# A Mamba-2 and mixture-of-experts layer on one core: moved loads, copies and waits at four joints between its stages

## The reference

```python
y = mamba2_mixer(x * (1 + sc1) + sh1, ...)             # ends in y_normed (2048 x 2048) @ w_out
x = layer_norm(ALPHA * x + (1 + g1) * y, g, b)
hm = x * (1 + sc2) + sh2
probs = softmax(hm @ w_router + b_router)              # 32 experts in 4 groups, the best group, its top 2
y = sum over the 2 chosen: gate * (silu(hm @ w_gate[e]) * (hm @ w_up[e])) @ w_down[e]
out = layer_norm(ALPHA * x + (1 + g2) * y, g, b)
```

## Time and profile before

| | |
|---|---|
| median of 3 runs | 2968.27 us (2964.40 to 2972.89) |
| profiled execution | 2967.99 us, span 2966.2 us, mean granted clock 0.973 |
| busy | PE 94%, PEld 79%, DVE 74%, POOL 49%, ACT 44% |
| mixer | to 1541 us |
| projection and norm | 1541 to 1933 us |
| router and tables | 1933 to 2010 us |
| experts | 2010 to 2870 us |
| output | 2870 to 2966 us |
| chain that ended last | PE 76%, DVE 11%, issue 4%, DMA 3% of the span |

### The profile page before, as it was taken

The page is one execution under the profiler, slowest core; times in us unless marked ns, Lnnn a source line. Parts: engine busy times, 40 slices in busy tenths (PEclk is TensorE's granted clock), DMA queues, the critical chain, the costliest instruction groups (busy, mean ns, idle before and its releaser), DMA issues.

```text
span 2966.2 us, 41186 instructions
## 1 busy us (share of the span) xinstructions
PE 2775.1 (94%) x14699; PEld 2333.7 (79%) x14699; DVE 2194.2 (74%) x2633; ACT 1309.1 (44%) x1671; POOL 1467.3 (49%) x753
## 2 busy tenths in 40 slices
PE   3899999999999999999988999948999999999986
PEld 2688888888888888888876888846888888888852
DVE  7678777787878778787764333385888888888867
ACT  4534333333433333343431111125777777777743
POOL 0133433333343343333432222214899999999974
PEclk9999999999999999999998999968999999999989
DMA  8854545444553544454352222239887869668768
GB/s 267 311 183 155 213 146 182 178 160 174 185 209 127 204 173 144 182 198 167 111 184 96 106 105 103 82 121 339 320 317 259 307 242 362 244 234 303 268 235 332
DMA packets 253183, 610.11 MB, mean 206 GB/s; under 512 B 15968, under 2 KB 98560, under 8 KB 244864
## 3 DMA queue, kind: packets, MB, share of 16 engines
q1 hardware_dynamic: 228208, 525.26, 49.6%
q0 software_dynamic: 11520, 41.95, 3.8%
q10 hardware_dynamic: 13328, 41.21, 3.4%
HBM read 600.75 MB, written 99.89 MB: 236 GB/s over the span
## 4 chain that ended last, share of the span: by engine, by line
PE 76%; DVE 11%; issue 4%; DMA 3%; POOL 2%; ACT 2%; SPq 1%; ACTq 0%; POOLq 0%; DVEq 0%
PE op L691 18%; PE pz L706 11%; PE op L1697 10%; PE gp_e L2124 9%; PE yp L2124 9%; PE up_e L2124 9%; DVE cv L1227 3%; PE yi L750 3%; PE yx L753 2%; PE op L2116 1%; PE sbp L758 1%; PE tx L769 1%; DVE decay L1264 1%; PE tx L723 1%; PE lgP L1722 1%
## 5 line engine op out<-in xcount | busy, mean ns | idle before, releaser
L2072 DVE TENSOR_TENSOR piece_lo<-piece_raw,piece_hi 128x2048 fp32r<-128x2048 f32 x186 | 552.1, 2987 | 119.8 <-ACT piece_hi L2181 119.7
L2181 ACT CAST piece_hi<-piece_raw 128x2048 fp32r<-128x2048 f32 x274 | 515.6, 1913 | 191.1 <-issue 78.9
L691 PE MATMUL op<-hm,w_hi 128*128 128x512 f32 x2048 | 532.3, 405 | 45.9 <-DVE hm L1353 45.9
L2072 POOL TENSOR_TENSOR piece_lo<-piece_raw,piece_hi 128x2048 fp32r<-128x2048 f32 x91 | 552.0, 6067 | 44.1 <-ACT piece_hi L2181 42.8
L1227 DVE SCALAR_TENSOR_TENSOR cv<-ub,par,cv 128x512 f32<-128x512 f32 x384 | 381.1, 993 | 154.0 <-ACT cv L950 144.8
L691 PEld LDWEIGHTS op<-hm,w_hi 128*128 128x128 f32 x2048 | 379.0, 190 | 120.1 <-DVE hm L1353 45.9
L641 POOL TENSOR_TENSOR xw<-xw,t 128x512 f32<-128x512 f32 x64 | 98.7, 1543 | 490.5 <-DVE t L1295 490.5
L706 PE MATMUL pz<-wz_hi,hm 128*128 128x256 f32 x2048 | 296.6, 290 | 1.1 <-DVE wz_lo L1205 0.4
L706 PEld LDWEIGHTS pz<-wz_hi,hm 128*128 128x128 f32 x2048 | 266.5, 192 | 7.3 <-DVE wz_lo L1205 3.9
L691 PE MATMUL op<-hm,w_lo 128*128 128x512 f32 x1024 | 254.9, 391 | 0.0
L622 POOL TENSOR_TENSOR xdt<-xw,tab 128x512 f32<-128x512 f32 x64 | 70.4, 1099 | 367.6 <-ACT xw L969 345.8
(11 more groups left out here) (344 smaller groups left out, 5755.3 us busy)
## 6 DMA issues: line engine op xcount, KB each, us to landing
hm<-hm_parts SPq DMA_DIRECT2D x30, 4096.0 KB, 14.0
piece_raw<-in_w_gate SPq DMA_DIRECT2D x94, 1024.0 KB
piece_raw<-in_w_up SPq DMA_DIRECT2D x94, 1024.0 KB
piece_raw<-in_w_down SPq DMA_DIRECT2D x92, 1024.0 KB
decay<-acum_rows SPq DMA_DIRECT2D x32, 1024.0 KB, 4.7
w_raw<-in_w_in SPq DMA_DIRECT2D x48, 512.0 KB, 6.0
expert_out<-ye ACTq DMA_DIRECT2D x46, 512.0 KB, 6.6
w_ada_part<-in_w_ada_t SPq DMA_DIRECT2D x32, 512.0 KB, 3.9
```

Of the source, the lines that this page charges most:

```text
L691: mm = nc.tensor.matmul(pj[m % 2][:], wp[m][:, kk, :], hm[b][:, hp, kk, :], start=q == 0, stop=q == 3 * KK - 1)
L2072: v.tensor_tensor(lo[q][:], raw[q][:], hi[q][:].bitcast(F32), ALU.subtract).then_inc(lo_done[q], 1)
L2181: nc.scalar.copy(hi[q][:], raw[q][:]).then_inc(hi_done[q], 1)
```

## The change

It has five edits.

1. SP issues `load_y(2, 0)` inside the mixer's list, behind the issue of the last y stores; step 1 of the projection loads only the second half. DVE runs `mix_rows` between the two low parts of tile 2.
2. ACT's `power(0, EARLY)` stands ahead of the wait for `lg_mm`.
3. DVE makes `ids`, `tile_expert` and `fresh` ahead of the low parts 3 and 4 of tile 0, and 3, 4 and 5 behind them.
4. The first two fetches gather by the column of `ids` itself, with no copy into `ix`; from tile 2 on the copy stays.
5. `xa` has 16 buffers, in the places of the raw and high pieces 0 to 3, `ya` moves to memory below. SP loads `xa1` to `xa8` as the low parts 0 to 3 of the tile behind the last come, and 9 to 15 behind these, and the output stage loads none. DVE waits for 8 to 15 once, at tile 8.

```diff
@@ output_buffers
+    w.ya = [sb(f"ya{n}", [P, D]) for n in range(OUT_RING)]
+    sb("unused14", [P, 440])
...
-    xa = [sb(f"xa{n}", [P, D]) for n in range(1, OUT_RING)]
+    xa = [sb(f"xa{n}", [P, D]) for n in range(1, TT)]
     sb("unused16", [P, D])
-    w.ya = [sb(f"ya{n}", [P, D]) for n in range(OUT_RING)]
...
+    w.xa_late = sem("xa_late")
@@ mixer_steps, sync
             store(LAST, 1)
+            for h in range(2):
+                sp.wait_ge(y_stored[h], 32 * (STEPS - SPANS + 2))
+            load_y(2, 0)
             sp.wait_ge(zero_out, 16 * GROUPS)
@@ out_projection, sync
-            if in_loop(i, 1, TT - 1):
+            if in_loop(i, 2, TT - 1):
                 load_y(i + 1, 0)
@@ out_projection, scalar
+                if isinstance(j, int) and j == TT - 2:
+                    power(0, EARLY)
                 if in_loop(j, 1, TT):
                     act.wait_ge(lg_mm, j)
-                if isinstance(j, int) and j == TT - 2:
-                    power(0, EARLY)
@@ out_projection, vector
-                low(i + 1, 1 - b)
+                low_half(i + 1, 1 - b, 0)
                 mix_rows()
+                low_half(i + 1, 1 - b, 1)
@@ experts, sync
-        for n in range(1, OUT_RING):
-
-            if n % 2:
-                sp.wait_ge(lo_done[(n - 1) // 2], 2 * last + 3)
-                sp.sem_inc(k.passed, 1)
-            sp.dma_start(w.xa[n][:], k.xad[n]).then_inc(w.xa_in[n], 16)
+        for q in range(GU):
+            sp.wait_ge(lo_done[q], 2 * last + 3)
+            sp.sem_inc(k.passed, 1)
+            for n in (2 * q + 1, 2 * q + 2):
+                sp.dma_start(w.xa[n][:], k.xad[n]).then_inc(w.xa_in[n] if n < OUT_RING else w.xa_late, 16)
+        for n in range(OUT_RING + 1, TT):
+            sp.dma_start(w.xa[n][:], k.xad[n]).then_inc(w.xa_late, 16)
@@ experts, gpsimd, fetch
-            nc.gpsimd.tensor_copy(ix[b][:], k.ids[:, bass.ds(t, 1)]).then_inc(ix_ready, 1)
-            pool.wait_ge(ix_ready, t + 1)
-            pool.sem_inc(k.passed, 1)
+                nc.gpsimd.tensor_copy(ix[b][:], k.ids[:, bass.ds(t, 1)]).then_inc(ix_ready, 1)
+                pool.wait_ge(ix_ready, t - 1)
+                pool.sem_inc(k.passed, 1)
+            rows = ix[b][:] if in_loop(t, 2) else k.ids[:, t:t + 1]
@@ experts, vector
-        low_part(dve, nc.vector, 3, 0)
-        low_part(dve, nc.vector, 4, 0)
         dve.wait_ge(ids_mm, 1)
...
-        low_part(dve, nc.vector, 5, 0)
+        for q in range(3, PIECES):
+            low_part(dve, nc.vector, q, 0)
@@ output, sync
-            if i + R < TT:
-                load(i + R)
@@ output, vector
-            dve.wait_ge(xa_in[s], 16 * (i // R + 1))
+            if i < R:
+                dve.wait_ge(xa_in[i], 16)
+            elif i == R:
+                dve.wait_ge(w.xa_late, 16 * (TT - R))
```

More of the change, by code:

```diff
@@ L265, in output_buffers @@
     w.ve = sb("ve2", [P, 1])
-    sb("unused14", [P, 11192 - 2 * D - 4 * P])
+    w.ya = [sb(f"ya{n}", [P, D]) for n in range(OUT_RING)]
+    sb("unused14", [P, 440])
     w.dga, w.dgb = ([sb(f"{n}{b}", [P, P]) for b in range(2)] for n in ("diag_a", "diag_b"))
@@ L2080, in fetch @@
                 pool.sem_inc(k.passed, 1)
-            nc.gpsimd.tensor_copy(ix[b][:], k.ids[:, bass.ds(t, 1)]).then_inc(ix_ready, 1)
-            pool.wait_ge(ix_ready, t + 1)
-            pool.sem_inc(k.passed, 1)
+                nc.gpsimd.tensor_copy(ix[b][:], k.ids[:, bass.ds(t, 1)]).then_inc(ix_ready, 1)
+                pool.wait_ge(ix_ready, t - 1)
+                pool.sem_inc(k.passed, 1)
+            rows = ix[b][:] if in_loop(t, 2) else k.ids[:, t:t + 1]
             nc.gpsimd.indirect_dma_start(out=xg[b][:], out_offset=None, in_=k.h2d[:],
-                                         in_offset=bass.IndirectOffsetOnAxis(ap=ix[b][:], axis=0)
+                                         in_offset=bass.IndirectOffsetOnAxis(ap=rows, axis=0)
                                          ).then_inc(x_in[b], 16)
@@ L2373, in _ @@
     def _(sp):
-        def load(i):
-            sp.wait_ge(r_done, i - R + 1)
-            sp.dma_start(xa[i % R][:], k.xad[i]).then_inc(xa_in[i % R], 16)
         for i in range(TT):
@@ L2452, in summed @@
         def summed(i):
-            s, b = i % R, i % 2
+            b = i % 2
             dve.wait_ge(ms_done, i + 1)
-            dve.wait_ge(xa_in[s], 16 * (i // R + 1))
+            if i < R:
+                dve.wait_ge(xa_in[i], 16)
+            elif i == R:
+                dve.wait_ge(w.xa_late, 16 * (TT - R))
             if i >= 2:
@@ L2458, in summed @@
                 dve.wait_ge(nm_done, i - 1)
-            nc.vector.tensor_tensor_reduce(out=r[b][:], in0=both[b][:], in1=xa[s][:], scale=1.0, scalar=0.0,
+            nc.vector.tensor_tensor_reduce(out=r[b][:], in0=both[b][:], in1=xa[i][:], scale=1.0, scalar=0.0,
                                            op0=ALU.add, op1=ALU.add, accum_out=total[b][:]).then_inc(r_done, 1)
```

## The result

The changed kernel takes 2943.82 us (median of 4 runs, 2941.0 to 2945.99) against 2969.73 for the kernel before beside it (4 runs, 2964.4 to 2972.89): ratio 0.9914, 95% interval 0.9896 to 0.9932. The forecast was 2933, with 2943 as the end of its range, so the sign was right and the gain was too large: 35.5 us forecast, 25.9 measured. The profiled execution took 2942.14 us with a span of 2940.4, against 2967.99 and 2966.2 before.

The account below looks back on a forecast made before the run. TensorE was taken as busy throughout the projection and expert loops, with waits or transfers binding four other stretches. Gains of 10.8 + 9.0 + 6.7 + 9.0 = 35.5 us from 2967.99 gave 2933 us, range 2926 to 2943.

Parts of the forecast that it names:

- Part 1: Mixer's end: earlier load of y for tile 2 gains 10.8 us; bounds 9.0, and 12.6 if tile 3's slow start goes.
- Part 2: Router: exponential waits only for its own input, gaining 9.0 us (8.0 to 9.6); the rest becomes a wait for x.
- Part 3: First gather at the experts' start: earlier token table and no index copy give 6.85 us together, taken as 6.7.
- I expect it 0.8 us ahead of the first low part: Experts' start: GpSimd's first gather issue begins 0.8 us before VectorE's first low part, keeping the 6.7 us gain.
- GpSimd's first gather is locked out: Rival at the experts' start: the first gather gains 3.7 us instead of 6.7, total 2936 us; chance 8%.
- lower bound of 3.7 us: Experts' start: gain left if the first gather's issue falls behind one low part, starting at about 1999.1.
- Part 4: Expert loop: instructions stay but for one GpSimd register operation, costed at nothing; GpSimd's copies still 18.3 us apart.
- Part 5: Output stage: residual loads moved earlier gain net 9.0 us; bounds 5 and 10.9, the latter without delay.
- I take 4.3, the nearest row: all gathers start 1.7 us later: Output stage's head: last expert store lands in 4.3 us instead of 2.6, delaying all gathers by 1.7 us.
- VectorE becomes the bound: Output stage, tiles 4 to 15: transfers need 3.75 us a tile, VectorE 3.80, so 10.9 us go.
- the 16 residual tiles collide with the stage's head: Rival in the output stage: last store takes 6.7 us; 4 us later, period 4 us, total 2937 us; chance 8%.
- transfers stay the bound: Rival in the output stage: lower transfer rate, 4.4 us a tile, 6.6 us come back, total 2938 us; chance 3%.

Follow-up runs that it names:

- e3: Changed kernel with part 3 undone (two low parts ahead of the token table, one behind it, index copied by GpSimd): 2943.05 us, ratio 0.9927.
- e4: Changed kernel, VectorE's three low parts behind the token table waiting for a semaphore GpSimd raises behind its first two gathers: 2937.37 us, ratio 0.9909.
- e9: Changed kernel with output gathers issued five tiles ahead instead of four: 2939.05 us, ratio 0.9907.
- e13: Changed kernel without the eight late residual loads (part of the output wrong) and with output gathers five tiles ahead: 2938.4 us, ratio 0.9902.
- e6: Changed kernel without the eight late residual loads; tiles 8 to 15 add residual tiles 0 to 7 instead: 2942.85 us, ratio 0.992.
- e1: Changed kernel with part 1 undone (y for tile 2 loaded after all stores landed, both low halves ahead of row mixing): 2950.51 us, ratio 0.9957.
- e18: Changed kernel with VectorE's two slot copies moved ahead of the three low parts and output gathers five tiles ahead: 2934.01 us, ratio 0.9893.
- e14: Changed kernel with part 5 undone (eight residual tiles loaded inside the output stage, one a tile): 2947.44 us, ratio 0.9943.

## Why the prediction was right in its parts 1 and 2 and short in 3 and 5

**Part 1** was right in mechanism; the term was 10.8 us and measured 9.2 in this trace and 10.0 by the middle of 15. The early load was put down as landing 8.6 us after the store's issue and took 9.8 (1545.48 - 1535.72), the second half 3.72 us and took 4.64. What the term takes away was also less fixed than assumed: 5.6 us for the two stores in one trace, 7.7 in the other.

**Part 2** was right to its numbers: 9.0 us, a wait of 3.3 for x where some 4 were forecast.

**Part 3** failed at the step "I expect it 0.8 us ahead of the first low part". Its 0.4 us from table to issue left out a gap that stood in the earlier trace rows: 1.0 us between the end of the index copy and the issue. That gap belongs to the gather, not to the copy, and stayed: table to issue is 1.22 us. The low parts came where they were expected, 1.3 us behind the table. So the lead was 0.05 us, and the rival "GpSimd's first gather is locked out" (8%) came true, at over twice its price (7.2 us less, not 3.0): it was priced for one low part, since a held copy had cost 2.45 us, and the issue in fact stood for all three. That a short lead is not enough could be read before. In the kernel before, the low part beside that copy is this line of DVE's timeline:

```profile
1999.55 2.27 DVE L2072 TENSOR_TENSOR piece_lo<-piece_raw,piece_hi 128x2048 fp32r<-128x2048 f32 x1
```

The copy began at 1999.42, 0.13 us ahead of it, and still ended at 2001.87, 0.05 us behind its end, where it takes 0.19 us undisturbed; in e3 it is the same with 0.12 us. The Trainium skill (SBUF — State Buffer, Who interferes with whom) names the exclusive lock, and says that the one that starts first has it. By its row the first gather starts first in 17 traces and was held in 12 of them, so they agree only if the gather's hold begins later than its row does. The same section of the Trainium skill infers that a subtraction of this kind doesn't stop descriptors being made, and says also that one with two inputs in SBUF contends with a GpSimd instruction that reads SBUF, as this gather does for its index. The 7.81 against 1.22 us shows the issue held; whether it stands at the index or at the descriptors no run here tells. The lower bound of 3.7 us, meant as the worst case, excluded a loss without a reason. Of the 6.85 us the gap took 0.8, and e4 shows the rest: 6.0 us better than before.

**Part 4** was right: the loop took 862.6 us against 862.4.

**Part 5** failed at two terms. "I take 4.3, the nearest row: all gathers start 1.7 us later": the store took 6.5 us, and the gathers started 3.5 us later, 1.8 more than put down; it was close to the row of 6.7 in the earlier trace rows that had been left to the bound. And "VectorE becomes the bound": true for bandwidth, as e9 shows, but the period was compared with bytes alone. The landing of a tile's second gather (6.5 to 8.4 us in the changed kernel) against its lead was never set up as a term. It cost 2.8 us here (44.57 - 41.78). With both gone (e13) the stage brings 82.3 - 71.6 = 10.7 us, so the ideal 10.9 was right, but only for a kernel that leaves eight loads out; with all of them and the longer lead (e9) it brings 82.3 - 74.8 = 7.5. The rival "the 16 residual tiles collide with the stage's head" gave "4 us later, with a period of 4 us", which is what the trace shows; "transfers stay the bound" gives a similar period for a wrong reason, and only e6 and e9 tell them apart.

The sum: 35.5 forecast; 1.6 less in part 1, 7.2 in part 3, 4.3 in part 5, 0.2 in the loop make 22.4 - 0.2 = 22.2; a shorter mixer and the clock gave back 3.4, and 0.2 is left over, most of it in tile 3's start, 0.3 us earlier than part 1 and the mixer account for. The 3.4 us are luck. The clock's 1.5 stood in part 1's upper bound ("lose their slow start as well"), but they are not the early load's doing: with the same load the 48 matmuls took 11.4, 13.0 or 14.2 us from one trace to the next.

## What to carry to other kernels

When work is moved off a chain onto an engine beside it, look at who else needs a shared resource in the same tenths of a microsecond: here the price of a lead of 0.05 us was 6.6 us, and two 0.17 us copies bought it back. For a ring of prefetched buffers compare three numbers, not two: bytes per step over bandwidth, the consumer's pace, and lead minus landing time. Here removed loads that changed nothing (e6) pointed to the third, and a longer lead (e9) showed it. And a trace prices a part only by distances inside itself, since work ahead of the change moved by up to 4 us from one execution to another.

## What was not expected of the hardware

- A gather's issue by GpSimd that begins 0.04 to 0.05 us ahead of VectorE's subtractions in SBUF took 7.81 us in 12 of 12 traces; 0.28 to 0.45 us ahead, 1.22 us in 5 of 5. Where between 0.05 and 0.28 us it turns wasn't tried for a gather; an index copy that began 0.12 to 0.13 us ahead of a low part was held (before and e3, 2.45 us where it takes 0.19 undisturbed). The second gather, begun inside the first of three subtractions, took only 1.87 to 2.02 us, as though let in at the end of that one, while the held first gather wasn't let in between them. Why is open.
- A semaphore increment written behind an indirect transfer on GpSimd's queue ran 0.28 us after the transfer's issue began, not after its end (e4). It doesn't mark that the issue is over.
- Of 20 traces (before, changed and e1 to e18) tile 3's first 48 matmuls took 11.4 to 11.5 us in four, 12.9 to 13.0 in eleven and 14.2 to 14.3 in five, with edits that don't touch them. The granted clock (the third number from the end; the last two are DMA share and GB/s) shows it. First two windows of the changed kernel, whose TensorE had waited 0.84 us ahead of them, then of e4, where it had waited 1.61:

```profile
1594.00:1600.00 6.00, 5.16 (x31) 4.46 (x30) 3.34 (x4) 1.04 (x1) 0.00 (x0) 1.00 0.25 72
1600.00:1606.00 6.00, 6.00 (x27) 4.84 (x27) 3.77 (x8) 1.24 (x1) 0.86 (x2) 1.00 0.13 47
```

```profile
1594.00:1600.00 6.00, 4.38 (x13) 3.48 (x13) 4.95 (x7) 0.72 (x1) 0.00 (x0) 0.61 0.30 87
1600.00:1606.00 6.00, 6.00 (x23) 4.75 (x22) 2.95 (x5) 1.24 (x1) 2.67 (x2) 0.82 0.00 0
```

The first stays at 2.4 GHz (1.00); the second spends part of each window at 1.2 GHz. TensorE's idle time ahead does not sort the traces: 3.27 us gave 12.99 in e14, 1.61 gave 14.26 in e4, 1.66 gave 11.46 in e18. What sorts them stays open. It is 1.5 to 2.8 us of any comparison between single traces of this kernel.
